# Uneven token chunks, four index-query jobs left out, and index keys gathered across sequences, in a fused sparse-attention and HGRN2 step

## The chip, the core and the metric

The kernel runs as one program on one core of a Trainium2 chip. The metric is the device time of one execution in microseconds (us); lower is better. The core has TensorE (PE, matrix products; PEld is its weight loading), VectorE (DVE), ScalarE (ACT), GpSimd (POOL) and the queues that issue DMA transfers (SP's above all). Each engine works through its own list of instructions in a fixed order and waits at semaphores.

## What is computed

One step of a one-layer decoder on 1024 prompt tokens and 8 sample tokens (one for each of 8 sequences with 1024 past keys). A normalised input goes through one wide projection; its columns feed sparse attention, an index that picks 256 keys for each query, and a gated linear recurrence (HGRN2). The part that matters here:

```python
def indexer_topk(iq, iw, ik, q_pos, topk):
    s = jnp.einsum('bthd,bsd->bths', iq.astype(F32), ik.astype(F32)) * IDX_DIM ** -0.5
    score = jnp.einsum('bths,bth->bts', jax.nn.relu(s), iw)
    ...
    score = jnp.where(causal[None], score, -jnp.inf)
    _, idx = lax.top_k(score, topk)          # topk = 256
    valid = idx <= q_pos[None, :, None]
    return idx, valid
```

A prompt query at position below 256 has at most 256 visible keys, so all of them are kept whatever their scores are: its index query is never used. The sample tokens' index queries are used, against keys that are gathered page by page from `cache_ik` through `page_table`.

## The kernel before, in words

**Units and jobs.** The 4168 columns of the projection are cut into 17 units of at most 256 columns (`UNITS`): unit 0 is `ix` (index keys and weights, 72 columns), units 1 and 2 are `iq` (index queries, 4 heads each), unit 3 is the first half of `gh`, unit 4 the first `hg` (gate and query of two HGRN2 heads), and so on. The weights of a unit arrive by DMA (`w_raw`), ACT writes their rounded high part (`high_w`, tile `w_high`), POOL the rest (`split_w`, tile `w_low`), and every product is three matrix products: high with high, high with low, low with high. PE works through *jobs*: one job is 24 matmuls (8 slices of the 1024 inputs, three products) into one PSUM bank. A job of form "T" has the columns of the projection on partitions and a *chunk* of tokens as its moving columns; form "N" has one row tile of 128 tokens on partitions and 256 columns of the projection moving; form "S" does the 8 sample tokens of the next unit (64 small matmuls). `ix`, `iq` and `hg` are computed in form T; an `iq` or `hg` unit has two halves `b` of 128 columns, each over the three chunks of `CHUNKS`.

**The front.** The input rows `x_rows` (9 tiles: 8 of 128 tokens and the sample tokens as tile 8) are loaded by SP. For each group of tiles ACT sums the squares (`squares`), DVE works out the roots in a chain of eleven small instructions (`x_roots`), DVE and ACT scale the rows (`scale_rows`), PE transposes them (`transpose_x`, L2150), ACT copies the high part out of PSUM (`high_x`) and DVE the low part (`low_x`). `X_AT` says within which job PE transposes which slices of the next chunk. `FRONT` lists the jobs of group 0, in which `ix` and the first `iq` unit alternate chunk by chunk. `IX_JOBS` is the number of jobs after which the last `ix` job is done: the weights of unit 2 take the place of those of unit 0, so `high_w(2)` waits for it.

**Index items.** An item (`ITEMS`) is one row tile t = 2 to 7 of queries, one head h: PE multiplies with all keys up to t (2 or 4 matmuls, L2214), ACT applies relu (`index_relu`), DVE weighs and adds to `scores` (`add_scores`). Two PSUM buffers and two relu buffers alternate. There are 48 items in 12 groups of four; `GROUPS` says behind which job a group is done: on PE its four items are spread over the job that follows. After all items and a causal mask on POOL (`affine_select`), DVE searches the 256th largest score bit by bit in 31 rounds; the loop that follows on DVE takes the sample tokens' search in between.

**POOL's list at the start** is: `split_w(0)`, `split_w(1)`, then the 32 gathers of index keys (`load_index_keys`: sequence pair `bp` = 0 to 3, page `g` = 0 to 7, 64 KB each) with `split_w(2)` and `split_w(3)` among them, then six causal masks, `split_w(4)` and the later units. Each gather waits until the one before it *of the same pair* has landed:

```python
for g in range(g0, g1):
    ge(gp, s[f"index_pages_in{bp}"], 16 * g)
```

PE begins a unit only when its whole low part is there:

```python
elif u not in begun:
    begun.add(u)
    pe.wait_ge(s["weights_low_ready"], 2 * u + 2)
```

A job also waits until the one that used its bank before has been copied out (`job_copied`). The product with the gathered keys (`sample_index`, L2240) is behind job `SAMPLE_AT`, the sum over heads (`sample_index_sum`, L2248) behind `SAMPLE_SUM_AT`. Later events (`FLAGS_AT`, `EVENTS` with the recurrence's chunks) are placed by job number too.

## Time and profile before

| | us |
|---|---|
| median of 3 runs (lowest, highest) | 805.73 (801.14, 806.96) |
| profiled execution, device time | 804.48 |
| its span, first to last instruction | 802.8 |
| PE busy | 760.7 |
| DVE busy | 542.8 |
| ACT busy | 420.7 |
| POOL busy | 396.2 |

The device time lies 1.7 us above the span; what is added to the span is added to it. A wait on an engine counts only where the chain that ends last passes through it.

### The profile page before, as it was taken

The page shows a single profiled execution, that of the slowest core. Times are in us where ns is not written, and L with a number is a line of the kernel's source. Part 1 is how long each engine was busy: PE and PEld are TensorE (multiplying, and loading weights), DVE is VectorE, ACT ScalarE, POOL GpSimd, SP SyncE. Part 2 cuts the span into 40 slices and gives each one's busy share as a digit, 9 for nine tenths or more (in the row PEclk, how much of TensorE's full clock was granted, in tenths as well). Part 3 has the DMA queues.
Part 4 walks back from the last instruction along what each step waited for, and adds up shares of the span by engine and source line. Part 5 has one row for each costly group of instructions (what it writes and reads, how often), then busy time and mean ns, then how long its engine had stood idle before and what let it go on. Part 6 is the DMA issues. An engine that isn't in the chain of part 4 may idle for free.

```text
span 802.8 us, 20221 instructions
## 1 busy us (share of the span) xinstructions
PE 760.7 (95%) x7576; PEld 704.1 (88%) x7576; DVE 542.8 (68%) x1110; ACT 420.7 (52%) x1274; POOL 396.2 (49%) x576
## 2 busy tenths in 40 slices
PE   3999999999999999999989999979799998999998
PEld 3889989899999999999988999868588878898998
DVE  3644767998999999879994846678446367555121
ACT  6765775346365686577554746554435554422110
POOL 3454735437735693579396435249932427510220
PEclk9999999999999999999999999999999999999999
...
GB/s 282 93 21 86 14 90 41 66 66 42 53 3 80 94 47 74 80 95 47 74 28 75 124 127 166 161 253 134 155 153 140 206 122 142 124 139 55 229 101 82
DMA packets 69927, 83.57 MB, mean 104 GB/s; under 512 B 20458, under 2 KB 55962, under 8 KB 69578
## 3 DMA queue, kind: packets, MB, share of 16 engines
...
## 4 chain that ended last, share of the span: by engine, by line
PE 76%; POOL 8%; DVE 5%; issue 4%; ACT 4%; DMA 2%; POOLq 0%; SPq 0%; ACTq 0%; DVEq 0%
PE psum L2298 25%; PE psum L2295 16%; PE psum L1331 11%; PE psum L2214 3%; PE psum L1264 3%; PE psum L1280 3%; POOL w_low L549 2%; PE psum L2172 2%; PE psum L2191 1%; PE psum L1242 1%; PE psum L1238 1%; PE psum L2150 1%; PE psum L1244 1%; DMA page_keys<-in_cache_kt 1%; POOL page_keys L613 1%
## 5 line engine op out<-in xcount | busy, mean ns | idle before, releaser
L2298 PE MATMUL psum<-w_high,xT_high 128*128 128x256 f32 x640 | 183.2, 286 | 0.3 <-ACT stage L1804 0.3
L2298 PE MATMUL psum<-w_low,xT_high 128*128 128x256 f32 x640 | 179.8, 281 | 0.0
L2298 PE MATMUL psum<-w_high,xT_low 128*128 128x256 f32 x640 | 179.6, 281 | 0.0
L549 POOL TENSOR_TENSOR w_low<-w_raw,w_high 128x256 fp32r<-128x256 f32 (+1 forms) x144 | 105.5, 769 | 65.0 <-ACT w_high L1686 54.7
L2298 PEld LDWEIGHTS psum<-w_high,xT_high 128*128 128x128 f32 x640 | 120.4, 188 | 2.4 <-ACT stage L1804 0.5
L2298 PEld LDWEIGHTS psum<-w_high,xT_low 128*128 128x128 f32 x640 | 120.5, 188 | 0.4
L2298 PEld LDWEIGHTS psum<-w_low,xT_high 128*128 128x128 f32 x640 | 120.6, 188 | 0.0
L2295 PE MATMUL psum<-xT_high,w_high 128*128 128x384 f32 (+3 forms) x312 | 103.8, 333 | 0.9 <-POOL w_low L549 0.9
L2295 PE MATMUL psum<-xT_high,w_low 128*128 128x384 f32 (+3 forms) x312 | 100.3, 322 | 0.0
L2295 PE MATMUL psum<-xT_low,w_high 128*128 128x384 f32 (+3 forms) x312 | 100.3, 322 | 0.0
L2037 DVE TENSOR_SCALAR_CACHE_REDUCE flag_count<-scores,candidate 128x512 f16<-128x512 f32 (+2 forms) x96 | 96.9, 1009 | 0.0
L2037 DVE TENSOR_SCALAR_CACHE_REDUCE flag<-scores,candidate 128x384 f16<-128x384 f32 (+2 forms) x96 | 84.1, 876 | 9.2 <-DVE candidate L2053 8.6
L914 ACT ACTIVATE prob<-psum,neg_max 128x1024 f32<-128x1024 f32 (+7 forms) x64 | 47.4, 740 | 67.6 <-DVE neg_max L1172 67.4
L1331 PE MATMUL psum<-w_high,xT_high 128*128 128x256 f32 x256 | 73.3, 286 | 0.1
L1331 PE MATMUL psum<-w_low,xT_high 128*128 128x256 f32 x256 | 71.9, 281 | 0.0
L1331 PE MATMUL psum<-w_high,xT_low 128*128 128x256 f32 x256 | 71.8, 281 | 0.0
L1576 POOL DMA_INDIRECT index_keys_T<-in_cache_ikt,index_page_rows x32 | 34.8, 1088 | 56.1 <-DMA index_keys_T<-in_cache_ikt,index_page_rows 54.8
L2295 PEld LDWEIGHTS psum<-xT_high,w_high 128*128 128x128 f32 (+1 forms) x312 | 58.4, 187 | 3.7 <-POOL w_low L549 1.4
L2295 PEld LDWEIGHTS psum<-xT_low,w_high 128*128 128x128 f32 (+1 forms) x312 | 58.3, 187 | 0.7
L1172 DVE CUSTOM_DVE_ANT_0 psum<-psum,mask 128x1024 f32<-128x1024 f32 (+5 forms) x48 | 43.0, 898 | 23.5 <-PE psum L1244 23.3
L2295 PEld LDWEIGHTS psum<-xT_high,w_low 128*128 128x128 f32 (+1 forms) x312 | 58.1, 186 | 0.5
L1804 ACT ACTIVATE stage<-psum 128x256 f32<-128x256 f32 x64 | 24.7, 387 | 57.6 <-PE psum L2298 53.5
...
## 6 DMA issues: line engine op xcount, KB each, us to landing
...
```

The source lines that it names most:

```text
L549: last = gp.tensor_tensor(WL[:, u % 2, 4 * h + k, 0:w], raw(u)[:, h, k, 0:w], f(WH[:, u % 2, 4 * h + k, 0:w]), ALU.subtract)
L914: act.activation(PB[:, m % 3, 0:w], ps(2 * (m % 2), w), ACT.Exp, scale=-1.0, bias=NB[:, h:h + 1], accum_out=RS[:, t % 2, h:h + 1]).then_in ...
L1172: dve.tensor_tensor_reduce(lg, lg, mask, -HD ** -0.5, 3e38, ALU.add, ALU.min, accum_out=NB[:, h:h + 1])\
L1264: last = pe.transpose(ps(4, P, o=b * P), PB[:, m % 3, b * P:(b + 1) * P], IDN[:, :])
L1280: last = pe.matmul(ps(7, P, (g + 1) * HD, g * HD, kv * P), VT[:, b, kv * HD:(kv + 1) * HD], PTS[(2 * p + g) % 3][:, b, :], start=b == 0, s ...
L1331: last = pe.matmul(ps(OBANK[y], UW, rows(i)), a[:, k, row0(i):row0(i) + rows(i)], ww[:, sl, k, :], start=k == 0 and a is XH and ww is WH, ...
L1576: gp.indirect_dma_start(dst, None, cache_ikt.rearrange("a d k -> (a d) k"), bass.IndirectOffsetOnAxis(ap=PGX[:, col:col + 1], axis=0))\
L1804: last = act.activation(STG[0:r, (g + 1) % 4, :], ps(bank, UW, r), fn)
L2037: dve.tensor_scalar((JK, CU)[k % 2][:, 0:w], sc, threshold(k), None, op, ALU.add, accum_out=CNT[:, k:k + 1]).then_inc(s["dve_chain"], 1)
L2214: last = pe.matmul(ps(4 + 2 * (m % 2) + c0 // 512, w), IQS[:, h, (t - 2) * P:(t - 1) * P], stack[:, c0:c0 + w], start=kk == 0, stop=kk == 1)
L2295: last = pe.matmul(ps(BANK[n], cw, m_), ww[:, sl, k, i * P:i * P + m_], x[:, k, t0:t0 + cw], start=first, stop=final)
L2298: last = pe.matmul(ps(BANK[n], w, rows(i)), x[:, k, row0(i):row0(i) + rows(i)], ww[:, sl, k, 0:w], start=first, stop=final)
```

## The change

`CHUNKS` goes from 384, 384 and 264 tokens (the last with the 8 sample tokens) to 256, 384 and 392. The row tiles are grouped 2, 3 and 4 (`CHUNK_ROWS`), with one tile of each group scaled by ACT. The first chunk now holds only tokens whose index queries are never used, so `FRONT` and the `iq` unit skip it: four jobs of 24 matmuls fewer, jobs 2 lower in number after the front and 4 lower after unit 2. All tables of job numbers are moved; `GROUPS` starts behind job 6 instead of 8. `sample_index` is behind job 20 instead of 22, which is now the first job of unit 4 and was the seventh of unit 3. All tiles of the second chunk are transposed in one go behind job 0. SP loads the second group of rows ahead of the weights of unit 1. POOL's gathers are in another order: pages 0 to 2 of the pairs 0, 1, 2 in turn; after `split_w(2)` pages 0 to 2 of pair 3; then pages 3 to 7 of all four pairs in turn; `split_w(3)` behind them all.

```diff
@@ -51,7 +51,9 @@
-CHUNKS = [(0, 384), (384, 384), (768, 264)]
+CHUNKS = [(0, 256), (256, 384), (640, 392)]
+CHUNK_ROWS = [(0, 1), (2, 3, 4), (5, 6, 7, 8)]
+ROWS_BY_ACT = (1, 4, 7)
 UNITS = [("ix", 0), ("iq", 0), ("iq", 1), ("gh", 0), ("hg", 0), ("hv", 0), ("hv", 1),
@@ -83,11 +85,11 @@
-FRONT = [(x, b, c) for c in range(3) for x, b in ((0, 0), (1, 0), (1, 1))]
-IX_JOBS = 7
+FRONT = [(x, b, c) for c in range(3) for x, b in ((0, 0), (1, 0), (1, 1)) if x == 0 or c > 0]
+IX_JOBS = 5
 SAMPLE_UNITS = [u for u in range(3, NU) if UNITS[u][0] != "hg"]
...
-X_AT = {(2, 3): (1, range(4)), (2, 7): (1, range(4, 8)), (4, 7): (2, range(4)), (5, 3): (2, range(4, 8))}
+X_AT = {(0, 7): (1, range(8)), (3, 3): (2, range(4)), (3, 7): (2, range(4, 8))}
@@ -102,7 +104,7 @@
     if kind == "iq":
-        out = [(u, "T", b, c) for c in range(3) for b in range(2)]
+        out = [(u, "T", b, c) for c in (1, 2) for b in range(2)]
         return out + [(u + 1, "S", NT, 0)] if u == 2 else out
@@ -121,25 +123,25 @@
     JOB0.append(JOB0[-1] + len(jobs(_u)))
-LOWS = JOB0[2] + 6
+LOWS = JOB0[2] + 4
 ORDERED = [job for _u in range(NU) for job in jobs(_u)]
...
 ITEMS = [(t, 4 * half + h) for half in range(2) for t in range(2, NT) for h in range(4)]
-GROUPS = {8: [0], 9: [1], 10: [2], 11: [3], 12: [4], 13: [5, 6], 15: [7], 16: [8], 17: [9], 18: [10], 19: [11]}
+GROUPS = {6: [0], 7: [1], 8: [2], 9: [3, 4], 11: [5], 12: [6], 13: [7], 14: [8], 15: [9], 16: [10], 17: [11]}
 ITEMS_AT = {n: [4 * g + x for g in gs for x in range(4)] for n, gs in GROUPS.items()}
-KEYS_ROWS_AT, SAMPLE_AT, SAMPLE_SUM_AT = 7, 22, 23
-
-FLAGS_AT = {29: 0, 36: 1, 42: 2, 46: 3, 49: 4, 53: 5, 72: 6, 77: 7}
+KEYS_ROWS_AT, SAMPLE_AT, SAMPLE_SUM_AT = 5, 20, 21
+
+FLAGS_AT = {25: 0, 32: 1, 38: 2, 42: 3, 45: 4, 49: 5, 68: 6, 73: 7}
 KEEP_AT = [4, 6, 8, 10, 12, 14, 23, 26]
...
-    chunk = t // 3
-    return max(IX_JOBS, (3, 6, 9)[chunk] if h < 4 else JOB0[2] + 2 * chunk + 2)
+    c = 1 if t < 5 else 2
+    return max(IX_JOBS, (4, 7)[c - 1] if h < 4 else JOB0[2] + 2 * c)
@@ -1436,15 +1438,15 @@
             def load_x(g):
-                for i in range(3 * g, 3 * g + 3):
+                for i in CHUNK_ROWS[g]:
                     sp.dma_start(x_buf(i)[0:rows(i)], x_rows(i)).then_inc(s[f"x_in{i}"], 16)
...
             sp.dma_start(LG[:, :], bass.AP(ln_g.tensor, 0, [[1, P], [P, KC]]), allow_slow_non_contiguous=True).then_inc(s["gain_in"], 16)
+            load_x(1)
             load_weights(sp, 1)
-            load_x(1)
             load_x(2)
@@ -1565,11 +1567,9 @@
-            def load_index_keys(bp, g0, g1):
-
-                if bp == 3:
-                    gp.wait_ge(s["x_transposed"], 2 * KC)
-                for g in range(g0, g1):
+            def load_index_keys(g0, g1, bps):
+
+                for g, bp in [(g, bp) for g in range(g0, g1) for bp in bps]:
                     ge(gp, s[f"index_pages_in{bp}"], 16 * g)
@@ -1581,26 +1581,23 @@
                 link(gp.iota(ROWN[hh * HD:(hh + 1) * HD, :], [[0, SB // 2 * NPG]], base=0, channel_multiplier=1))
-            gp.wait_ge(s["x_rows_scaled"], 2)
             split_w(gp, 0)
...
             link(gp.tensor_tensor(PGX[:, :], PGX[:, :], ROWN[:, :], ALU.add))
-            load_index_keys(0, 0, NPG)
+            load_index_keys(0, 3, range(3))
             gp.wait_ge(s["const_in"], CONSTS_IN)
...
             gp.tensor_scalar(TRI[:, P:2 * P], TRF[:, :], 1.0, 0.0, ALU.mult, ALU.add)
-            load_index_keys(1, 0, 3)
             gp.wait_ge(s["x_low_ready"], 3 * KC)
...
             split_w(gp, 2)
-            load_index_keys(1, 3, NPG)
-            load_index_keys(2, 0, 3)
+            gp.wait_ge(s["x_transposed"], 3 * KC)
+            load_index_keys(0, 3, (3,))
+            load_index_keys(3, NPG, range(4))
             split_w(gp, 3)
-            load_index_keys(2, 3, NPG)
-            load_index_keys(3, 0, NPG)
             for u in range(2, NU):
@@ -1653,7 +1650,7 @@
-                act.wait_ge(s["x_roots_ready"], i // 3 + 1)
+                act.wait_ge(s["x_roots_ready"], ROWS_BY_ACT.index(i) + 1)
                 act.activation(x_buf(i), x_buf(i), ACT.Copy, scale=STAT[:, 3, i:i + 1]).then_inc(s["x_rows_scaled_act"], 1)
@@ -1768,7 +1765,7 @@
                                     iqp[b2 * HD:(b2 + 1) * HD, 8 * b2 + 2 * j + hh:4 * BR:BR + 16],
-                                    ps(bank, SB, (hh + 1) * HD, hh * HD, 256)[:, b2:SB:2], ACT.Copy)
+                                    ps(bank, SB, (hh + 1) * HD, hh * HD, T - t0)[:, b2:SB:2], ACT.Copy)
                 elif kind == "ix":
@@ -1841,16 +1838,16 @@
             act.activation(RS[:, 0, 0:1], CNT[:, 0:1], ACT.Square)
-            for i in range(3):
+            for i in range(2):
                 squares(i)
             high_w(0)
-            scale_rows(2)
+            scale_rows(1)
             act.wait_ge(s["gain_in"], 16)
-            high_x(0, range(4))
+            high_x(0, range(KC))
+            for i in range(2, 5):
+                squares(i)
             high_w(1)
-            high_x(0, range(4, KC))
-            for i in range(3, 6):
-                squares(i)
+            scale_rows(4)
             for u in (0, *range(2, NU)):
@@ -1859,25 +1856,22 @@
                     if n == 1:
-                        for i in (6, 7):
+                        for i in range(5, NT + 1):
                             squares(i)
-                        scale_rows(5)
-                    if n == 2:
-                        squares(NT)
+                    if n == IX_JOBS - 1:
+                        high_w(2)
                     if (n, 3) in X_AT:
...
                     evac(u, q)
-                    if n == 3:
+                    if n == 1:
                         scale_rows(7)
...
                         high_w(u + 1)
-                    if n == IX_JOBS - 1:
-                        high_w(2)
                     if n == KEYS_ROWS_AT:
@@ -1931,8 +1925,8 @@
             def x_roots(g):
-                c = slice(3 * g, 3 * g + 3)
-                dve.wait_ge(s["x_squares_ready"], 3 * g + 3)
+                c = slice(CHUNK_ROWS[g][0], CHUNK_ROWS[g][-1] + 1)
+                dve.wait_ge(s["x_squares_ready"], CHUNK_ROWS[g][-1] + 1)
                 x, y, tmp = STAT[:, 1, c], STAT[:, 3, c], STAT[:, 2, c]
@@ -2071,27 +2065,26 @@
             x_roots(0)
-            for i in (0, 1):
-                scale_rows(i)
+            scale_rows(0)
             dve.wait_ge(s["gain_in"], 16)
...
             x_roots(1)
-            for i in (3, 4):
+            for i in (2, 3):
                 scale_rows(i)
...
                         low_x(*X_AT[n, 3])
+                    if n == 1:
+                        x_roots(2)
+                        for x in (5, 6, NT):
+                            scale_rows(x)
                     if n < LOWS:
...
                     if n == 2:
-                        x_roots(2)
-                        for x in (6, NT):
-                            scale_rows(x)
-                    if n == 4:
                         constants()
@@ -2140,12 +2133,12 @@
                     pe.wait_ge(s["ident_in"], 16)
-                pe.wait_ge(s["x_rows_scaled"], 2 * c + 2)
+                pe.wait_ge(s["x_rows_scaled"], (1, 3, 6)[c])
                 pe.wait_ge(s["x_rows_scaled_act"], c + 1)
...
                         pe.wait_ge(s["x_low_ready"], KC * c + k - 3 if c > 0 else 1)
-                    for i in range(3 * c, 3 * c + 3):
+                    for i in CHUNK_ROWS[c]:
                         r = rows(i)
```

POOL at the start of the program, from its first `split_w` (`w_low`) on. `x8` is one `split_w`; `index_keys_T_140` is the tile of pair 3. Before:

```order
L549 TENSOR_TENSOR w_low<-w_raw,w_high 128x72 x8
L549 TENSOR_TENSOR w_low<-w_raw_146,w_high 128x256 x8
...
L1576 DMA index_keys_T<-in_cache_ikt,index_page_rows 128x128 x8
...
L1576 DMA index_keys_T<-in_cache_ikt,index_page_rows 128x128 x3
L1597 TENSOR_TENSOR x_sample_T<-xT_high,xT_low 128x64
L549 TENSOR_TENSOR w_low<-w_raw,w_high 128x256 x8
L1576 DMA index_keys_T<-in_cache_ikt,index_page_rows 128x128 x8
L549 TENSOR_TENSOR w_low<-w_raw,w_high 128x256 x8
L1576 DMA index_keys_T<-in_cache_ikt,index_page_rows 128x128 x5
L1576 DMA index_keys_T_140<-in_cache_ikt,index_page_rows 128x128 x8
L1611 AFFINE_SELECT scores<-scores 128x128 x6
```

And now, from the same place:

```order
L1576 DMA index_keys_T<-in_cache_ikt,index_page_rows 128x128 x9
...
L1595 TENSOR_TENSOR x_sample_T<-xT_high,xT_low 128x64
L551 TENSOR_TENSOR w_low<-w_raw,w_high 128x256 x8
L1576 DMA index_keys_T_140<-in_cache_ikt,index_page_rows 128x128 x3
L1576 DMA index_keys_T<-in_cache_ikt,index_page_rows 128x128 x3
L1576 DMA index_keys_T_140<-in_cache_ikt,index_page_rows 128x128
...
L551 TENSOR_TENSOR w_low<-w_raw,w_high 128x256 x8
L1608 AFFINE_SELECT scores<-scores 128x128 x6
L551 TENSOR_TENSOR w_low<-w_raw,w_high 128x256 x16
```

Between `split_w(2)` and `split_w(3)` stood 8 gathers and now stand 23; none is left behind `split_w(3)`.

PE from the last index item (t = 7, 4 matmuls) to the start of unit 4, whose first job is the one that waits for `weights_low_ready`. Before:

```order
686 L2214 MATMUL psum<-ikT_high_low_144,iqT_stack_143 128x512 [waits index_relu_ready,index_low_ready]
...
693 L2298 MATMUL psum<-w_high_113,xT_high_102 128x256 [waits job_copied]
...
744 L2240 MATMUL psum<-index_keys_T_180,iq_padded_181 64x512 [waits index_pages_in1]
...
753 L2298 MATMUL psum<-w_high_113,xT_high_102 128x256 [waits job_copied]
...
777 L2248 MATMUL psum<-relu_sample_182,index_weight_sel_97 128x512 [waits index_weights_selected,sample_index_relu]
...
780 L2295 MATMUL psum<-xT_high_102,w_high_113 128x384 [waits job_copied,weights_low_ready]
```

And now:

```order
638 L2207 MATMUL psum<-ikT_high_low_144,iqT_stack_143 128x512 [waits index_relu_ready,index_low_ready]
...
645 L2291 MATMUL psum<-w_high_113,xT_high_102 128x256 [waits job_copied]
...
669 L2288 MATMUL psum<-xT_high_102,w_high_113 128x256 [waits job_copied,weights_low_ready]
...
696 L2233 MATMUL psum<-index_keys_T_180,iq_padded_181 64x512 [waits index_pages_in1]
```

Between the last item's rest of a job and unit 4 stood three jobs, `sample_index` and its sum; now one job stands there, and the other two jobs are ahead of the last item.

## Rows read from the trace of the kernel before

**Rows 1.** The page: the chain that ended last, by engine.

```profile
PE 76%; POOL 8%; DVE 5%; issue 4%; ACT 4%; DMA 2%; POOLq 0%; SPq 0%; ACTq 0%; DVEq 0%
```

**Rows 2.** Waits of PE, 0 to 160 us: in total, times, longest.

```profile
PE psum L2150 <- DVE x_rows L1950: 13.1, 1, 13.1
PE psum L2214 <- ACT relu L1834: 1.9, 4, 0.8
PE psum L2295 <- POOL w_low L549: 0.9, 2, 0.6
```

**Rows 3.** The chain in order of time, 0 to 160 us: start, duration, what.

```profile
34.45 8.38 PE psum L2295 x48
42.84 1.94 PE psum L2150 x12
...
54.27 0.26 issue
...
62.07 0.80 PE psum L2295 x3
...
64.67 0.35 PE psum L2214 x2
...
76.67 0.64 PE psum L2214 x4
...
88.70 0.81 PE psum L2214 x4
...
134.06 0.93 PE psum L2214 x4
134.99 6.04 PE psum L2298 x51
```

**Rows 4.** Timeline, 0 to 55 us: start, duration, instruction, [idle before].

```profile
5.67 1.06 ACT L1651 ACTIVATE square_junk<-x_rows 128x1024 bf16<-128x1024 f32 x1
...
9.36 0.17 DVE L1937 TENSOR_SCALAR x_stats<-x_stats 128x3 f32<-128x3 f32 x1 [7.81 <-ACT square_junk L1651]
...
11.54 1.15 ACT L1657 ACTIVATE x_rows<-x_rows,x_stats 128x1024 f32<-128x1024 f32 x1 [1.64 <-DVE x_stats L1942]
11.54 1.42 DVE L1950 TENSOR_SCALAR x_rows<-x_rows,x_stats 128x1024 f32<-128x1024 f32 x2
...
13.06 5.34 PE L2150 MATMUL psum<-ident,x_rows 128*128 128x128 f32 x24 [13.06 <-DVE x_rows L1950]
...
18.07 0.51 PE L2295 MATMUL psum<-xT_high,w_high 128*72 128x384 f32 x1
...
43.88 1.59 ACT L1664 ACTIVATE xT_high<-psum,ln_gain 128x264 fp32r<-128x264 f32 x4
```

**Rows 5.** Timeline of POOL, 45 to 140 us and from 128 us.

```profile
76.36 0.94 POOL L1576 DMA_INDIRECT index_keys_T<-in_cache_ikt,index_page_rows  x1 [1.75 <-DMA index_keys_T<-in_cache_ikt,index_page_rows]
77.61 0.94 POOL L1576 DMA_INDIRECT index_keys_T<-in_cache_ikt,index_page_rows  x1 [0.31 <-issue]
80.27 1.25 POOL L1576 DMA_INDIRECT index_keys_T<-in_cache_ikt,index_page_rows  x1 [1.71 <-DMA index_keys_T<-in_cache_ikt,index_page_rows]
...
84.17 9.60 POOL L549 TENSOR_TENSOR w_low<-w_raw,w_high 128x256 fp32r<-128x256 f32 x8
...
137.77 5.59 POOL L549 TENSOR_TENSOR w_low<-w_raw,w_high 128x256 fp32r<-128x256 f32 x8
```

**Rows 6.** Groups of POOL by shape, 20 to 135 us: the gathers.

```profile
L1576 POOL DMA_INDIRECT index_keys_T<-in_cache_ikt,index_page_rows x32 | 34.8, 1088 | 56.1 <-DMA index_keys_T<-in_cache_ikt,index_page_rows 54.8 <-issue 1.1 <-POOL index_page_rows L1589 0.3
```

**Rows 7.** Timeline of PE, 574 to 590 us, around a wait for a DMA.

```profile
579.36 1.93 PE L1358 MATMUL psum<-page_keys,q_padded 128*32 128x256 f32 x16 [4.36 <-DMA page_keys<-in_cache_kt]
...
583.95 0.41 PE L1242 MATMUL psum<-bias_high,antidiagonal_r 128*128 128x256 f32 x1
584.16 0.42 PE L1242 MATMUL psum<-bias_low,antidiagonal_r 128*128 128x256 f32 x1
```

**Rows 8.** Stretches of 3 us: busy time of PE, PEld, DVE, ACT, POOL, then granted clock, DMA share, GB/s.

```profile
582.00:585.00 3.00, 3.00 (x15) 2.46 (x17) 0.62 (x2) 0.60 (x1) 0.00 (x0) 0.52 0.09 23
```

## The prediction

> **What bounds the kernel now.** First the page's chain: PE carries 76% of it, POOL 8% [rows 1]. Then PE's waits in the first 160 us, where the change lies: one of 13.1 us at the start, 1.9 us for relus, 0.9 us for POOL's low weights [rows 2]. So after the start PE runs through, and what counts is PE's own work plus any wait that the change makes. The last reading is the chain in order of time [rows 3], which gives PE's pace and two marks. Pace: 48 matmuls of 384 columns in 8.38 us are 0.175 us each; 51 of 256 columns in 6.04 us are 0.118 us. So columns are paid for, at (0.175 - 0.118)/128 = 0.00045 us each, and one of 392 will take 0.178 us. A job is 24 of them: 2.8 us at 256, 4.2 at 384, 4.3 at 392. Marks: the last `ix` job ends at 54.3 us, and the seventh job of unit 3 at 141.0 us (134.99 + 6.04) [rows 3].
>
> **The removed jobs and the new widths.** Four jobs of 24 matmuls are gone. The chunks still sum to 1032 columns, so the `hg` units cost what they did (two jobs of 0.175 us and one of 0.12 before; one each of 0.118, 0.175 and 0.178 now, within 0.1 us a half). The `iq` units lose 256 columns in each of four halves: 4 x 24 x 0.118 = 11.3 us of PE's work. That is the gain on offer, and what follows takes it back.
>
> **The front.** Durations from [rows 4]. The first two tiles' squares end at 6.8 us. The roots take 2.2 us (9.36 to 11.54), the scaled row 1.15 us: PE's transposes start at 10.2 instead of 13.1 us. ACT copies 8 slices of 256 columns at 0.4 us (four of 264 in 1.59) to 14.2. Now the cover is missing: before, three jobs of the first chunk (12.6 us) lay over the squares, roots and scales of the next tiles; now one 256-column job does. Three squares (1.24 us each) end at 18.0, `high_w(1)` goes beside the roots (20.2), the two DVE scales end at 21.6. PE waits some 4 us for that. The 24 transposes then take 5.0 us if they run as the first 24 did (13.06 to 18.07), 2.9 us at the pace of the sixteen in 1.94 us [rows 3]; I take the slow one, as PE comes out of a wait in both: 26.6. Job 1 ends at 30.8, jobs 2 and 3 at 39.2, with two blocks of 16 transposes (1.94 us each) 43.1, and the last `ix` job at J = 47.4 us. Before it was 54.3 with two more jobs (8.4 us) ahead of it, so the front itself has lost 1.5 us. POOL's low weights of unit 1 are ready near 25 us, ahead of job 2. Bounds for this: 2.1 us less with quick transposes, 3 us more if a landing is late.
>
> **From J to unit 3, on PE.** Jobs 5 and 6 take 8.6 us and the transposed index rows between them 1.6 (54.27 to 62.07 less two jobs of 5.9 us and a wait of 0.3). `high_w(2)` and `split_w(2)` need 1.1 + 5.6 us and are covered by these 10.2. Unit 2 has two jobs of 384 and two of 392 columns, 17.0 us. One item costs 0.35 us at t = 2, 0.64 at t = 4, 0.81 at t = 6 and 0.93 at t = 7 [rows 3]; the sizes step evenly, so four heads of t = 2 to 6 are 11.8 us. The S job adds 1.0, small products 0.2, and 0.7 us goes where ACT copies a 392-column job ahead of the relus. PE asks for unit 3 at J + 10.2 + 17.0 + 11.8 + 1.9 = J + 40.9.
>
> **The same stretch on POOL.** `split_w(2)` ends at J + 6.7. Three gathers of pair 3 follow one after another; a gather alone is 0.94 us of issue and 1.75 us until it lands, 2.7 to 2.8 us [rows 5], so J + 13.4. Then 20 gathers over four pairs. Their waits are for a gather issued four earlier, so I take them as hidden: the pair at 76.36 and 77.61 overlapped, the second landed as soon as if alone [rows 5]. What is left is the issue, 1.09 us in the mean of 32 [rows 6], and 0.31 us between two [rows 5]: 1.36 us with the 1.05 of this stretch, 27.2 us together, J + 40.6. `split_w(3)` takes 5.6 us where DVE does not add scores (137.77) and 9.6 where it does (84.17) [rows 5]. PE's stall lets DVE run dry, so 5.7: J + 46.3. PE waits 5.4 us. The gathers' own waits, some 50 us of POOL's [rows 6], were off the chain in the kernel before, so taking them away earns nothing by itself; moving 15 more gathers ahead of `split_w(3)` is what counts. Ends: 0 if a gather takes 1.0 us, 13 us if each takes 1.55 and the split 9.6.
>
> **The clock after a wait.** After a wait of 4.36 us PE's 256-column matmuls start 0.21 us apart (583.95, 584.16) [rows 7], and the granted clock up to 585 us is 0.52, the level of 1.2 GHz [rows 8]. From 579.4 to 585 PE did about half of what 0.118 us a matmul gives, so such a wait costs some 2.5 us more. I add 2.5. The Trainium skill, "TensorE: Matmul & The Clock Gate", section "HAM oscillation — how this bites in real kernels", says that waits between bursts of matmuls put the array back to 1.2 GHz at each of them; by that rule both waits of this forecast pay, and the trace agrees with its 0.52.
>
> **Unit 3 to its seventh job.** PE starts at 47.4 + 46.3 = 93.7. Seven N jobs are 19.8 us, the items of t = 7 and of the second half 3.7 + 15.4, and 1.1 us is lost where `high_w(4)` (2.0 us) lies between two groups of relus on ACT. With 2.5 us for the clock: 136.2, against 141.0 before: 4.8 us ahead.
>
> **The start of unit 4.** `split_w(4)` is behind the causal masks, and these are behind the last scores. Before, the last item left PE at 134.99 and `split_w(4)` ended at 143.36 (137.77 + 5.59) [rows 3, 5]: 8.4 us, hidden by three jobs, `sample_index` and its sum. Now only 27 matmuls of 256 columns, 3.2 us, are in between; PE waits 5.2 us, and 2.5 go to the clock. Ends: 3 us with no clock loss, 9 us if the masks come late. 4.8 - 7.7 = **2.9 us slower**. Beside it: `sample_index` moved two jobs later still finds all gathers landed (J + 41); the DVE search keeps its distance to PE within 0.5 us (two N jobs later, 5.2 us of wait), so flags, scans and the recurrence stay where they were; the shorter first `hg` job sits where POOL paces the recurrence, and I take 0, ends -2 and +2 us.
>
> **The sum** against the profiled execution: 804.5 + 2.9 = 807.4 us. The median of the three runs is 1.2 us above that execution, so I say **808 us**. A measurement tells about 1% (8 us) from no change.
>
> **Rivals.** (1) The gathers are quick or the front loses less, and `split_w(3)` is on time; unit 4 still waits. For it: 1.25 us a gather, the smallest seen, saves 2.2 of the 5.4 us, and below some length the wait may leave the clock up. 807.4 - 5.4 - 2.5 = 799.5 us. (2) Neither wait appears: 799.5 - 7.7 = 791.8 us. Against it stands that the span from last item to low weights is made of a relu, a score, a mask and eight subtractions, all of fixed length, so it needs PE itself to run later than I think. (3) Slower: DVE holds POOL up. It decides from about 5 us more on POOL. The split at 84.17 took 4.0 us longer beside the scores than the one at 137.77 [rows 5], and gathers issued there take up to 1.25 us and more; at 1.55 us a gather 20 of them are 3.8 us more. 807.4 + 4.0 + 3.8 = 815.2 us. Against it: scores end when PE stands. The Trainium skill, "SBUF — State Buffer", section "Who interferes with whom", says that a DVE instruction with two SBUF inputs contends with a GpSimd instruction that reads SBUF; the scores are of that kind, and the 9.6 against 5.6 us agrees. By it the long split is the one to take if scores are still running. (4) That the change doesn't do what it says is excluded: the order of instructions has the four jobs less.
>
> **How the numbers follow.** Forecast 0.50, rival 1 0.18, rival 2 0.14, rival 3 0.18. The range reaches from rival 1 less 1.5 us to rival 3: 798 to 815 us, leaving out rival 2 and little else. Faster by over 1% (under 797.7): rival 2 and a bit, 0.15. Slower by over 1% (over 813.8): rival 3 and the tail of the forecast, 0.21. Same: 0.64.
>
> **What would show it.** In PE's waits after the change: one on DVE's scaled rows after job 0 of about 4 us, one for `w_low` before unit 3 of 5 us and one before unit 4 of 5 us, each with a granted clock near 0.5 behind it; POOL's gathers 1.25 to 1.5 us apart with no waits for landing; the last `ix` job ending near 47 us, the seventh job of unit 3 near 136. Wrong would be: gathers that run one at a time in spite of the order (20 at 2.7 us put unit 3 27 us later and the time near 830), or an end of the items so late that `split_w(4)` is hidden.

## The result, and the profile after

The changed kernel takes **819.05 us** (median of 4 runs, 816.25 to 824.24), the kernel before 804.91 in the same session: ratio 1.0188, 95% interval 1.0144 to 1.0231. The forecast was 808 us with a range up to 815: wrong in size, and beyond its range. Every trace is of one execution. The executions of one kernel differ by some microseconds (here 5.8 us from fastest to slowest before, 8.0 us after), so marks inside one trace are compared to tenths of a microsecond, but whole times only by the medians and their intervals. The profiled execution has a span of 816.8 us (before 802.8). Its chain, and TensorE's waits over the whole span (in total, times, longest):

```profile
PE 60%; DVE 15%; issue 9%; POOL 6%; ACT 6%; another core or an unknown queue 2%; DMA 1%; SPq 0%; DVEq 0%; ACTq 0%; POOLq 0%
```

```profile
PE psum L2207 <- ACT relu L1831: 14.5, 5, 7.2
PE psum L2143 <- ACT x_rows L1654: 11.5, 1, 11.5
PE psum L2143 <- DVE x_rows L1944: 7.6, 1, 7.6
PE psum L2288 <- POOL w_low L551: 5.2, 1, 5.2
PE psum L2291 <- ACT psum L1806: 4.8, 3, 3.3
```

Against [rows 1] and [rows 2]: the one front wait of 13.1 us has become two, 19.1 us; the relus cost 14.5 us in place of 1.9; the wait for unit 4's low weights is there as forecast (5.2); the forecast one ahead of unit 3 is not.

**The front.** VectorE's roots and scales of the second chunk (timeline of DVE: start, duration):

```profile
20.00 0.16 DVE L1936 SCALAR_TENSOR_TENSOR x_stats<-x_stats 128x3 f32<-128x3 f32 x1
20.20 0.74 DVE L1934 TENSOR_TENSOR x_stats<-x_stats 128x3 f32<-128x3 f32 x1
20.97 0.65 DVE L1935 SCALAR_TENSOR_TENSOR x_stats<-x_stats 128x3 f32<-128x3 f32 x1
...
24.38 2.31 DVE L1944 TENSOR_SCALAR x_rows<-x_rows,x_stats 128x1024 f32<-128x1024 f32 x2
```

The same kind of instruction takes 0.16 us at 20.00 and 0.65 behind it: GpSimd's split of unit 1 starts at 20.19 and runs to 26.1. The two scales take 2.31 us where two took 1.42 [rows 4]. The split of unit 1 in the kernel before, then in the changed one:

```profile
17.50 5.59 POOL L549 TENSOR_TENSOR w_low<-w_raw,w_high 128x256 fp32r<-128x256 f32 x8 [1.99 <-ACT w_high L1686]
```

```profile
20.19 5.95 POOL L551 TENSOR_TENSOR w_low<-w_raw,w_high 128x256 fp32r<-128x256 f32 x8 [10.24 <-ACT w_high L1683]
```

Both times it starts on ScalarE's `high_w(1)`. In the kernel before that stood ahead of the squares of the second group, and the split was over at 23.1, just ahead of the second group's roots at 23.80. The change puts it behind the squares, and the split now runs beside the roots.

**The hole.** ScalarE, then GpSimd, in the items of unit 2:

```profile
80.40 0.70 ACT L1831 ACTIVATE relu<-psum 128x640 f32<-128x640 f32 x1 [1.17 <-PE psum L2207]
89.57 0.70 ACT L1831 ACTIVATE relu<-psum 128x640 f32<-128x640 f32 x1 [8.46 <-remote]
98.08 1.30 ACT L1831 ACTIVATE relu<-psum 128x640 f32<-128x640 f32 x2 [7.80 <-remote]
```

```profile
79.96 0.94 POOL L1576 DMA_INDIRECT index_keys_T<-in_cache_ikt,index_page_rows  x1 [0.30 <-issue]
81.21 0.95 POOL L1576 DMA_INDIRECT index_keys_T<-in_cache_ikt,index_page_rows  x1 [0.30 <-issue]
...
93.72 0.94 POOL L1576 DMA_INDIRECT index_keys_T<-in_cache_ikt,index_page_rows  x1 [0.31 <-issue]
94.69 6.15 POOL L551 TENSOR_TENSOR w_low<-w_raw,w_high 128x256 fp32r<-128x256 f32 x8
```

The relu at 89.57 needs the item's products (TensorE left them at 79.2) and a free relu buffer, that is the score two items back (VectorE, before 78). Both had long come, and "remote" says that the profile knows no releaser. The same at 98.08. All that went on was GpSimd's gathers, 1.25 us apart, with no wait between them. I call this stretch the hole. The stretches (busy time of PE, PEld, DVE, ACT, POOL, granted clock, DMA share, GB/s):

```profile
64.00:80.00 16.00, 16.00 (x89) 14.93 (x88) 8.92 (x20) 9.63 (x20) 10.15 (x11) 1.00 0.19 51
80.00:82.00 2.00, 1.12 (x8) 0.74 (x6) 0.99 (x2) 0.70 (x1) 1.70 (x2) 1.00 0.22 66
82.00:90.00 8.00, 1.25 (x8) 0.92 (x6) 0.00 (x0) 0.43 (x1) 5.87 (x8) 0.74 0.19 51
90.00:94.00 4.00, 3.58 (x10) 2.91 (x10) 0.88 (x1) 0.27 (x1) 3.08 (x4) 0.50 0.17 49
94.00:98.00 4.00, 0.00 (x0) 0.00 (x0) 0.00 (x0) 0.00 (x0) 3.98 (x6) 0.50 0.11 33
```

TensorE, VectorE and ScalarE all stand for most of 18 us; the granted clock falls to 0.50, its 1.2 GHz level. The DMA share stays between 0.11 and 0.22.

**Unit 4.** The chain in order of time:

```profile
154.03 1.30 DVE scores L1996
155.75 5.49 POOL w_low L551 x8
161.29 4.45 PE psum L2288 x24
```

The last score, the split behind the last mask, then unit 4: the wait of 5.2 us, as worked out.

### The profile page after: what moved, and what is told of

Its sections match the earlier page's. It is cut to its first block, busy times and chain, and to the rows that moved or that the text cites. A ratio compares the mean times of both kernels' runs of the same rounds, so it can differ in the third digit from the quotient of the medians.

```text
span 816.8 us, 20008 instructions
## 1 busy us (share of the span) xinstructions
PE 752.3 (92%) x7480; PEld 695.5 (85%) x7480; DVE 556.9 (68%) x1102; ACT 420.3 (51%) x1266; POOL 387.7 (47%) x576
## 4 chain that ended last, share of the span: by engine, by line
PE 60%; DVE 15%; issue 9%; POOL 6%; ACT 6%; another core or an unknown queue 2%; DMA 1%; SPq 0%; DVEq 0%; ACTq 0%; POOLq 0%
PE psum L2291 14%; PE psum L1333 11%; PE psum L2288 10%; PE psum L2207 4%; PE psum L1266 4%; PE psum L1282 3%; DVE flag_count L2031 3%; POOL w_low L551 2%; DVE bit_kept L2044 2%; DVE flag L2031 2%; PE psum L1240 1%; PE psum L1246 1%; PE psum L1244 1%; POOL w_low L560 1%
## 5 line engine op out<-in xcount | busy, mean ns | idle before, releaser
L551 POOL TENSOR_TENSOR w_low<-w_raw,w_high 128x256 fp32r<-128x256 f32 (+1 forms) x144 | 102.9, 755 | 70.5 <-ACT w_high L1683 70.5
L2288 PE MATMUL psum<-xT_high,w_high 128*128 128x392 f32 (+5 forms) x280 | 95.9, 342 | 5.2 <-POOL w_low L551 5.2
L2288 PE MATMUL psum<-xT_low,w_high 128*128 128x392 f32 (+5 forms) x280 | 92.4, 330 | 0.0
L2288 PE MATMUL psum<-xT_high,w_low 128*128 128x392 f32 (+5 forms) x280 | 92.2, 329 | 0.0
L916 ACT ACTIVATE prob<-psum,neg_max 128x1024 f32<-128x1024 f32 (+7 forms) x64 | 47.4, 741 | 67.8 <-DVE neg_max L1174 67.6
L1996 DVE SCALAR_TENSOR_TENSOR scores<-relu,index_weight,scores 128x384 f32<-128x384 f32 (+5 forms) x42 | 40.8, 972 | 30.6 <-ACT relu L1831 29.3
L2288 PEld LDWEIGHTS psum<-xT_high,w_high 128*128 128x128 f32 (+1 forms) x280 | 53.2, 190 | 7.5 <-POOL w_low L551 5.4
L1683 ACT ACTIVATE w_high<-w_raw 128x1024 fp32r<-128x1024 f32 (+1 forms) x42 | 41.3, 1026 | 27.9 <-DMA w_raw<-in_w_main 19.2
L1831 ACT ACTIVATE relu<-psum 128x384 f32<-128x384 f32 (+5 forms) x48 | 35.7, 759 | 38.1 <-PE psum L2207 19.2
L2288 PEld LDWEIGHTS psum<-xT_low,w_high 128*128 128x128 f32 (+1 forms) x280 | 53.2, 190 | 0.7
```

The costliest lines, as they stand in the source:

```text
L551: last = gp.tensor_tensor(WL[:, u % 2, 4 * h + k, 0:w], raw(u)[:, h, k, 0:w], f(WH[:, u % 2, 4 * h + k, 0:w]), ALU.subtract)
L916: act.activation(PB[:, m % 3, 0:w], ps(2 * (m % 2), w), ACT.Exp, scale=-1.0, bias=NB[:, h:h + 1], accum_out=RS[:, t % 2, h:h + 1]).then_in ...
L1683: act.activation(WH[:, u % 2, 4 * h:4 * h + 4, 0:w], raw(u)[:, h, :, 0:w], ACT.Copy)\
L1831: act.activation(RB[:, m % 2, 0:w], ps(4 + 2 * (m % 2), w), ACT.Relu).then_inc(s["index_relu_ready"], 1)
L1996: ins = dve.scalar_tensor_tensor(sc, RB[:, m % 2, 0:w], IW[:, t, h:h + 1], sc, ALU.mult, ALU.add)
L2288: last = pe.matmul(ps(BANK[n], cw, m_), ww[:, sl, k, i * P:i * P + m_], x[:, k, t0:t0 + cw], start=first, stop=final)
```

## The experiments

Sixteen kernels, in four sessions; each ratio is to the kernel before in the same session, with its 95% interval. "Changed" is the changed kernel. The letters name the theories that each expectation states.

**1. Is it the gathers?** Three kernels: pace them; give back their old order; or put the new order alone into the kernel before.

```
# one at a time: changed, in load_index_keys
+ if g > 2 and bp > 0:
+     gp.wait_ge(s[f"index_pages_in{bp - 1}"], 16 * (g + 1))
+ if g > 3 and bp == 0:
+     gp.wait_ge(s["index_pages_in3"], 16 * g)
# old order: changed, with load_index_keys called at the places and with the pages of the kernel before
# by three: before, with load_index_keys and its calls as in the changed kernel
```

> The changed kernel with one thing added: each of the 20 gathers behind the three also waits until the gather issued before it has landed, so that one is in flight at a time, in the same order. Theory G (the run of gathers, issued 1.25 us apart without a pause, starves ScalarE: its relu stood 8.5 and 7.8 us with both of its semaphores long reached): the two waits of TensorE of 7.2 and 4.9 us on relu vanish. The gathers then take about 20 x 2.8 = 56 us from 65, so the last is issued near 121 and the split of unit 3's weights ends near 127, some 13 us behind the end of unit 2 at about 110: a new wait for w_low of unit 3 of 10 to 15 us. Time 815 to 823 us, no gain, but with the hole moved from 80 to 98 us to the start of unit 3. Theory C (the hole comes from the order of ScalarE's and VectorE's work under the new chunks, whatever GpSimd does): the relu waits stay at 14.5 us in all, and the time is about 819 us or more.

> The changed kernel with the old order and places of the gathers: eight of pair 0, three of pair 1, split of unit 2, five of pair 1, three of pair 2, split of unit 3, then the other 13, each waiting for the one before of its pair as before. The chunks and the left-out index queries stay. Theory G: no hole between 80 and 98 us, TensorE's relu waits fall from 14.5 to under 4 us, no new wait for unit 3's w_low (split of unit 3 ends near 90 us, unit 3 asks near 108). Time 802 to 808 us, near the kernel before: the 11.3 us of work removed less the later front. Theory C: the hole stays and the time is 815 to 821 us.

> The kernel before with the gathers' new order alone (three pages of three pairs at once, then after the split of unit 2 three of the last pair and 20 back to back, then the split of unit 3). Chunks and jobs as before. Theory G: the run of 20 lies at about 66 to 94 us, a hole of 8 to 16 us on ScalarE appears there and the time is 812 to 822 us. Theory C: no hole; split of unit 3 ends near 100 us, before it is wanted, and the time is 803 to 808 us as before.

Measured: one at a time 849.71 us (1.055, 1.0471 to 1.063); old order **805.72** (1.001, 0.9971 to 1.0049); by three alone **821.24** (1.0195, 1.0111 to 1.0279). TensorE's waits in the first 210 us with one at a time, and with the old order:

```profile
PE psum L2295 <- POOL w_low L551: 45.4, 1, 45.4
...
PE psum L2292 <- POOL w_low L551: 5.2, 1, 5.2
PE psum L2211 <- ACT relu L1835: 1.0, 1, 1.0
```

```profile
PE psum L2146 <- ACT x_rows L1657: 11.6, 1, 11.6
PE psum L2146 <- DVE x_rows L1947: 7.0, 1, 7.0
PE psum L2291 <- POOL w_low L551: 5.1, 1, 5.1
PE psum L2210 <- ACT relu L1834: 1.6, 2, 0.9
```

Paced or in the old order there is no hole. With the gathers' order alone on the kernel before, ScalarE stands as in the changed one:

```profile
88.27 0.70 ACT L1830 ACTIVATE relu<-psum 128x640 f32<-128x640 f32 x1 [4.99 <-remote]
93.20 0.48 ACT L1758 ACTIVATE iqT_stack<-psum 64x384 fp32r<-64x384 f32 x1 [4.22 <-remote]
...
100.94 1.51 ACT L1830 ACTIVATE relu<-psum 128x768 f32<-128x768 f32 x2 [6.76 <-remote]
```

So the gathers' order costs some 16 us alone, and the chunks with the left-out queries neither cost nor gain anything measurable. Theory G (the gathers do it) holds, and theory C (the order of work under the new chunks) is dead. My 815 to 823 for one at a time was far too low: a gather took 3.4 us in the mean from issue to issue, not 2.8, and TensorE, with no hole, asked for unit 3 at 94 us, not 110, so that the wait was 45.4 us and not 10 to 15.

**2. The front.** The split of unit 1 on GpSimd held back.

```
  split_w(gp, 0)
+ gp.wait_ge(s["x_rows_scaled"], 3)
  split_w(gp, 1)
```

> The changed kernel with the split of unit 1's weights on GpSimd held until the rows of group 1 are scaled, as it was held before the change. Theory P (GpSimd's split slows VectorE's small root instructions, 0.66 to 0.75 us each instead of 0.17, so the rows of the second chunk come at 26.7 us instead of 21.6): roots are back at 0.2 us, the rows are scaled near 22 to 23 us, TensorE's wait of 7.6 us falls to 3 to 4 us, and the time falls by 2 to 5 us, to 814 to 817. Rival: the split only moves later and unit 1's low weights come late, or the hole between 80 and 98 us takes up what is gained: time within 1 us of 819.

Measured: 817.15 us (1.0118, 1.0042 to 1.0193).

```profile
20.25 0.16 DVE L1935 TENSOR_TENSOR x_stats<-x_stats 128x3 f32<-128x3 f32 x1
...
21.43 1.42 DVE L1945 TENSOR_SCALAR x_rows<-x_rows,x_stats 128x1024 f32<-128x1024 f32 x2
```

The roots are back at 0.16 us, the scales at 1.42, the rows ready at 22.9 in place of 26.7; the wait is 4.9 us in place of 7.6, and the second chunk's jobs start at 28.3 us in place of 31.7. Theory P (the split slows VectorE's roots) holds for the place. The kernel's gain of 1.9 us is inside its scatter. The expectation calls this hold the one of the kernel before, and that is not so: there the split waited only for the first chunk's rows, scaled at 13.0 us [rows 4], and was early by ScalarE's order.

**3. What of the gathers makes the hole: landing, number, rate, bytes?**

```
# two in flight: changed, for the 20 gathers (g0 == 3)
+ if g0 == 3 and n > 1:
+     gp.wait_ge(s[f"index_pages_in{run[n - 2][1]}"], 16 * (run[n - 2][0] + 1))
# eight, split, twelve: changed
- load_index_keys(3, NPG, range(4)); split_w(gp, 3)
+ load_index_keys(3, 5, range(4)); split_w(gp, 3); load_index_keys(5, NPG, range(4))
# split first: changed, with split_w(gp, 3) ahead of the 23 late gathers
# plain copies: changed, for g > 2; the rows come from fixed places, so the page table is left out
- gp.indirect_dma_start(dst, None, ...)
+ gp.dma_start(dst, cache_ikt.rearrange("a d k -> (a d) k")[col * P:(col + 1) * P, :])
# spaced: changed, behind each of the 20
+ link(gp.tensor_scalar(ANR[:, :], ANT[:, :], 1.0, 0.0, ALU.mult, ALU.add))
```

> The changed kernel with each of the 20 gathers waiting until the gather two places before it has landed: two in flight where the changed kernel has up to four unwaited, and the run with one in flight had one. From the run with one in flight a gather takes about 3.25 us from issue to the next, so two in flight should come 1.6 to 2.0 us apart, 20 of them in 32 to 40 us, split of unit 3 ending near 108 to 114 us. Theory G1 (it is the rate of 1.25 us that starves ScalarE, and 1.6 to 2.0 us is slow enough): no idle stretch of ScalarE over 3 us with both semaphores reached; TensorE waits 12 to 20 us for w_low of unit 3 instead; time 820 to 828. Theory G2 (any gathers in flight while ScalarE works through the items do it): the hole stays and w_low is late too; time 825 to 840.

> The changed kernel with the split of unit 3's weights put into the run of gathers behind the first eleven (three of the last pair and eight), so that no run is longer than twelve. In the changed kernel and in the two others with the run of 20, ScalarE's first late start came after some 6 to 10 gathers of the run, and the nine gathers at 27 to 38 us made none. Theory G3 (the length of the run decides: something fills up over about ten gathers and empties in a pause): little or no hole, TensorE's waits on relu in all under 4 us, no wait for w_low of unit 3; time 804 to 809. Theory G4 (each gather costs ScalarE, wherever it is): the hole is cut in two parts of 6 to 8 us each and the time stays 815 to 820.

> The changed kernel with the split of unit 3's weights ahead of all 23 late gathers. The run of gathers then starts some 10 to 14 us later (near 75 to 80 us) and keeps its pace of 1.25 us. Theory G: the hole moves with the run, to some 88 to 108 us, and stays 12 to 16 us in all, in whichever items stand there; time 814 to 820 us. Theory C (something in the program of ScalarE at item 9 to 11 of the 24, not the gathers' time): the hole stays at items 9 to 11 near 80 to 98 us. If the gathers reach into the stretch where VectorE masks and sums the scores, the affine masks and the split of unit 4 are as late as before (wait of 5.2 us).

> The changed kernel with the 20 gathers of the run replaced by plain copies of as many bytes (128 rows of 512 B, 64 KB) issued by the same engine with the same waits; the rows come from fixed places instead of the index pages, so that the sample's index scores are computed from other pages. Theory D (the traffic of 64 KB per 1.25 us, 52 GB/s, or the DMA engines' share of 0.2 starves ScalarE): the hole stays, 815 to 820 us. Theory Q (GpSimd's own work of making the descriptors of an indirect gather does it, not the bytes): no hole; TensorE waits under 4 us on relu, the split of unit 3 starts earlier if a plain copy is issued faster than 1.25 us; time 803 to 808 us.

> The changed kernel with a small copy of 128x128 on GpSimd behind each of the 20 gathers (its duration was 0.32 us, with its completion awaited perhaps 0.45), which waits for nothing that a gather does: gathers some 1.7 us apart, as in the run with two in flight (35 us for 20, 1.75 each), but with no wait for a landing. Theory R (the rate of issue makes the hole: at 1.25 us ScalarE starved, at 1.75 it did not): no hole, and the split of unit 3 is late by some 8 to 14 us instead: time 812 to 817. Theory F (the number of gathers not yet waited for makes it, since only waits for a landing have removed it so far): the hole is there, of 8 us or more, and the time is 820 to 828.

| kernel | us | ratio, 95% interval | ScalarE's longest idle time with "remote" | TensorE's wait for unit 3's w_low |
|---|---|---|---|---|
| two in flight | 816.75 | 1.0166 (1.0094 to 1.0238) | 0.4 | 14.8 |
| eight, split, twelve | 809.18 | 1.0073 (1.0031 to 1.0116) | 7.3 | none |
| split first | 820.77 | 1.0209 (1.0126 to 1.0292) | 16.2 | none |
| plain copies | 806.71 | 1.0022 (0.998 to 1.0065) | none | none |
| spaced | 819.51 | 1.0204 (1.018 to 1.0228) | none | 15.4 |

Four of the five times missed the ranges of the theories that their traces bear out: two in flight came below 820 to 828, and eight, split, twelve, split first and spaced came 0.2, 0.8 and 2.5 us above theirs. What decides between the theories below is the hole in the trace, not the time.

Spaced, GpSimd's timeline: 1.8 us from gather to gather in the mean, and no gather waits for another to land.

```profile
81.08 0.98 POOL L1576 DMA_INDIRECT index_keys_T<-in_cache_ikt,index_page_rows  x1 [0.27 <-POOL antidiagonal_r L1580]
82.08 0.48 POOL L1580 TENSOR_SCALAR antidiagonal_r<-antidiagonal 128x128 fp32r<-128x128 f32 x1
82.84 0.98 POOL L1576 DMA_INDIRECT index_keys_T<-in_cache_ikt,index_page_rows  x1 [0.27 <-POOL antidiagonal_r L1580]
```

No hole, so it is the rate and not the count in flight (theory R over F), and two in flight (1.77 us in the mean) agrees. Plain copies, issued by the same engine to the same software queue, 20 in 13.4 us, bring more traffic at once and no hole:

```profile
64.00:80.00 16.00, 16.00 (x89) 14.92 (x88) 9.73 (x21) 10.64 (x22) 11.47 (x19) 1.00 0.33 90
80.00:100.00 20.00, 19.34 (x165) 16.99 (x164) 14.15 (x16) 15.05 (x30) 9.62 (x12) 1.00 0.20 61
```

So neither the bytes nor the queue by itself is it (Q over D); that it is the making of descriptors, as Q has it, no run isolates. One doubt stays: the copies were over in 13.4 us, and the gathers began to slow ScalarE and TensorE only some 8 to 13 us into a run, so a cause that goes by time and not by number is not excluded by this kernel. Splitting first moves the run to 82.8 to 110.2 us, and the hole moves with it, off the items where it was in the changed kernel. ScalarE, then TensorE, whose small matmuls (64 in 1.01 us in the chain of "one at a time") now come in handfuls every 0.72 us with nothing to wait for:

```profile
95.64 1.28 ACT L1799 ACT_TABLE_LOAD   x1
113.11 0.90 ACT L1799 ACTIVATE stage<-psum 8x64 f32<-8x64 f32 x4 [16.19 <-remote]
```

```profile
94.48 0.32 PE L2280 MATMUL psum<-w_raw,x_sample_T 128*8 128x64 f32 x4 [0.41 <-issue]
95.23 0.30 PE L2280 MATMUL psum<-w_raw,x_sample_T 128*8 128x64 f32 x4 [0.42 <-issue]
95.97 0.27 PE L2280 MATMUL psum<-w_raw,x_sample_T 128*8 128x64 f32 x3 [0.44 <-issue]
...
101.70 0.39 PE L2280 MATMUL psum<-w_raw,x_sample_T 128*8 128x64 f32 x3 [0.45 <-issue]
```

ScalarE's copy at 113.11 needs the last of these small matmuls, at 102.1. So of its 16.2 us of idle time 5.2 went on TensorE's own slowness, and it started 11.0 us late.

The length counts too. In "eight, split, twelve" the first nine in a row, the last issued at 77.8 us, cost nothing; in the twelve from 86.3 on, ScalarE stood from 96.4 until 103.67, 1.5 us behind the last. That is G3 (the length of the run) over G4 (each gather costs), with a run of twelve already too long.

**4. What was mended did not arrive.** From the old order: the split of unit 1 held; the split of unit 4 ahead of the last mask (`split_w(gp, u + 1)` at `t == NT - 1`, ahead of its wait); both.

> The kernel with the new chunks and the old order of gathers, with the split of unit 1 held until the rows of the second chunk are scaled. Theory P (in the run with the hold alone the rows were ready 3.8 us sooner, the wait of 7.6 us fell to 4.9, and the last index job of the front ended 3.2 us sooner; the kernel's time fell by only 1.9 us, inside its scatter): with no hole and no wait for unit 3's weights behind it, the 3 us arrive at unit 3's end; but unit 4 waits for its w_low by VectorE's scores (5.1 us). If VectorE's scores follow TensorE's earlier items, the whole moves: 802 to 803.5 us against 805.7. Rival: VectorE or ScalarE bounds the items and the 3 us are lost: 805 to 806.

> The kernel with the new chunks and the old order of gathers, with the split of unit 4's weights moved ahead of the last causal mask. The split then stands behind the fifth mask at 134.4 us and ends near 140.0, where unit 3's last job ends at 139.7; the last mask comes some 1 us later. Theory S (the wait of 5.1 us for w_low of unit 4, with a slower clock behind it, is time lost to the end): it falls to under 1 us and the time by 5 to 6 us, to 799.5 to 801. Rival (the search of the top keys on VectorE, which waits for the last mask, or a later wait takes it back): 803 to 806.

> The new chunks and the left-out index queries with the old order of gathers, the split of unit 1 held until the rows of the second chunk are scaled, and the split of unit 4 ahead of the last mask. If both gains add (3 and 5.5 us) the time is 796.5 to 799 us, 6 to 9 us under the kernel before, ratio 0.989 to 0.993. Rival: the gathers, which end at 131 us in the old order and stand ahead of the masks and of the split of unit 4, take the front's 3 us back, and the time is 799.5 to 801.

Measured: 806.42 (1.0044, 1.0028 to 1.0061), 807.67 (1.0066, 1.0041 to 1.0092), 809.52 (1.0072, 1.0042 to 1.0102). All three missed, and came out slower than even their rivals had it (806, 806 and 801 at most). Held, eleven gathers, nearly each behind the landing of the one before, stand between the split of unit 1 and that of unit 2, and TensorE waits 4.3 us for unit 2's low weights. With the split of unit 4 ahead of the mask, its wait is gone, but the split now runs beside the last four scores. These took 1.28 us each in the old order and take 10.90 together here (GpSimd and VectorE):

```profile
132.79 5.60 POOL L551 TENSOR_TENSOR w_low<-w_raw,w_high 128x256 fp32r<-128x256 f32 x8
```

```profile
132.75 10.90 DVE L2000 SCALAR_TENSOR_TENSOR scores<-relu,index_weight,scores 128x1024 f32<-128x1024 f32 x4 [0.57 <-ACT relu L1835]
```

So the last mask and VectorE's search come late, the search at 144.12 in place of 139.39, and TensorE waits for it. With all three it is the same (four scores in 10.89 us) and the search starts at 147.60:

```profile
144.12 0.55 DVE L2035 TENSOR_SCALAR_CACHE_REDUCE flag<-scores 128x384 f16<-128x384 f32 x1 [0.48 <-POOL scores L1613]
```

```profile
PE psum L2251 <- DVE enough L1001: 3.2, 3, 1.9
PE psum L2251 <- ACT hv L1796: 2.1, 1, 2.1
```

**5. Does the search set the time?** Short runs of gathers, with the splits between; items packed to end two jobs sooner, on three kernels.

```
# short runs: changed, with the split of unit 1 held
+ load_index_keys(3, 5, range(4)); split_w(gp, 3)
+ load_index_keys(5, 7, range(4)); split_w(gp, 4)      # no longer behind the masks
+ load_index_keys(7, NPG, range(4))
# early items: changed chunks
+ GROUPS = {6: [0], 7: [1], 8: [2], 9: [3, 4], 11: [5, 6], 12: [7], 13: [8, 9], 14: [10], 15: [11]}
# early items: kernel before
+ GROUPS = {8: [0], 9: [1], 10: [2, 3], 11: [4], 12: [5], 13: [6, 7], 15: [8, 9], 16: [10], 17: [11]}
```

> The changed kernel with GpSimd's queue mended in three places: the split of unit 1 held until the second chunk's rows are scaled; the run of 20 gathers cut into 8, 8 and 4 with the splits of unit 3 and of unit 4 between them; so no split behind the last mask. In every run so far VectorE's search began some 0.5 us behind the last mask, and the state updates of unit 6 on TensorE began 79 to 81 us behind it (before 137.84 to 216.8, old order 139.39 to 220.5, changed 155.79 to 235.7), whatever TensorE had gained or lost. Theory V (the end of the items sets the search's start and with it the time; no hole, no waits for w_low): items end 3 us sooner than with the old order, search begins near 136 to 137 us, time 800 to 803. Theory T (TensorE's own work sets the time): the 5.1 us for unit 4's w_low and 3 us of the front both arrive and the time is 796 to 798.

> The kernel with short runs of gathers, with the items also packed so that they end two jobs sooner (behind the job 15 in place of 17: two groups of four in one job twice). Theory V: items end some 5 to 6 us sooner (a job of unit 3 is 24 matmuls of 0.118 us, 2.8 us), search begins near 131 us, and the time falls by as much, to 795 to 798. Theory T, or ScalarE and VectorE cannot keep up with eight items in a job: no gain over the run without it, 800 to 803.

> The kernel before, with one thing changed: its items packed to end two jobs sooner (behind job 17 in place of 19). No work is taken away. Theory V: items end near 129 us in place of 135; the gathers, which end at 131.4 us ahead of the masks, let the search begin near 135 in place of 137.84, and the time falls by 2 to 3 us, to 800.5 to 802 against 803.5. Theory T: no change, within 1 us.

> The new chunks with the old order of gathers, and the items packed to end two jobs sooner. Theory V: the items end near 132 us in place of 138.9, the gathers end at 131.4, the search begins near 135.5 in place of 139.39, and the split of unit 4 ends near 141 in place of 144.8, so that TensorE waits 1 to 2 us for it in place of 5.1: the time falls by about 4 us from 805.7, to 801 to 803. Theory T: the wait for w_low alone counts, which falls by 3 to 4 us: about the same time, but then the early items of the kernel before gain nothing.

Measured: short runs **800.39** (0.9921, 0.9886 to 0.9956); with early items **799.34** (0.9927, 0.9896 to 0.9958); the kernel before with early items 803.92 (1.0002, 0.9978 to 1.0026); old order with early items 800.91 (0.996, 0.9933 to 0.9988). The first two are faster than the kernel before by 0.7 to 0.8%, the last by 0.4%; the early items add nothing measurable to the short runs. Marks of the profiled executions, in us: start of the last product of the index sum (TensorE), first flag of the search (VectorE), first product of the state updates (TensorE), span.

| kernel | sum | search | updates | span |
|---|---|---|---|---|
| before | 149.8 | 137.84 | 216.8 | 802.8 |
| before, early items | 152.7 | 135.35 | 219.7 | 801.9 |
| changed | 175.9 | 155.79 | 235.7 | 816.8 |
| old order | 160.7 | 139.39 | 220.5 | 805.7 |
| old order, early items | 157.7 | 138.69 | 217.5 | 799.1 |
| old order, split 4 early | 152.8 | 144.12 | 218.3 | 803.0 |
| all three of part 4 | 156.2 | 147.60 | 221.8 | 807.8 |
| short runs | 151.6 | 138.29 | 211.8 | 800.0 |
| short runs, early items | 154.2 | 135.15 | 213.9 | 794.8 |

Theory V (the search's start sets the time) falls as I had put it. On the kernel before the search starts 2.5 us sooner and the updates come 2.9 us later, as the sum does: TensorE sets them, 67.0 us behind the sum in both. In the new chunks (two jobs of unit 4 ahead of the sum) the distance is 59.7 to 59.8 us in four rows, and in the eight traces of such kernels that are not in the table. The two rows with the early split break it, at 65.5 and 65.6: there the updates come 74.2 us behind the search. So the updates start at about the later of sum + 59.8 and search + 74, a rule read off these marks and resting on two rows for its second half. Short runs stand on the edge (by the sum 211.4, by the search 212.3; found 211.8), with a visible wait for the search and one for ScalarE behind it:

```profile
PE psum L2294 <- ACT psum L1809: 3.9, 1, 3.9
PE psum L2250 <- DVE enough L1001: 3.6, 2, 2.7
```

From the updates to the end the rows differ by 7.3 us (580.9 to 588.2) with the same work. In the traces stand waits like these two, the one for `page_keys` (4.4 us before [rows 7], 3.5 in the old order, none in the changed kernel), with a slow clock behind them. These are single executions, and one kernel's own executions scatter as widely (short runs 791.31 to 807.0), so how much of this belongs to a kernel is not shown.

## Why the prediction was wrong, point by point

- **The removed jobs, 11.3 us:** right. TensorE has 96 matmuls less (x7480, before x7576).
- **The front, J = 47.4:** wrong, 53.6 measured (two jobs from 49.28 take 8.70 us, and it is the first). The step that failed is "the two DVE scales end at 21.6": they ended at 26.7, which is 5.1 of the 6.2 us. The forecast itself laid `high_w(1)` beside the roots and the low weights of unit 1 "near 25 us", so that the split ran across the roots and the scales, and it charged nothing for that. With the split held back the rows were ready at 22.9, so 3.8 us are the split's. The other 1.3 us came from the first chunk: its roots took 0.26 us each beside the split of unit 0, and its transposes began at 11.5 instead of 10.2. Another 0.9 us is a misreading: [rows 3] show 12 transposes in 1.94 us, and I took them for sixteen; the two blocks of sixteen took 2.38 us each. The Trainium skill, "SBUF — State Buffer", section "Who interferes with whom", says that VectorE contends with GpSimd's reads in an instruction with two SBUF inputs, and in tensor_scalar when it runs in its 2-port mode. The trace agrees for the first with 0.16 against 0.65 us; a tensor_scalar scale rose from 0.71 to 1.16, but no trace says in which mode it ran. I had used that rule for the long split only.
- **20 gathers on POOL:** the pace was 1.25 us, not 1.36, and none of the 20 waited; of the three ahead of them the first took 4.6 us until the next was issued, not 2.8. The split ended at 100.8, J + 47.2, against J + 46.3, so GpSimd's sum was right within 1 us. "PE waits 5.4 us" for unit 3 did not occur, since the hole made TensorE later than the split. By estimate it would have been some 7 us: one at a time, without a hole, TensorE asked for unit 3 at 93.9.
- **The step that failed for most of the miss:** the gathers' own waits were taken off as harmless ("taking them away earns nothing by itself"), at a price of nothing. They had spaced the gathers, and a run of some twenty without a pause stops ScalarE and TensorE. The old order against the changed kernel says what it costs: 15.2 us at the state updates, in place of my 7.9 us for unit 3's wait. At the seventh job of unit 3, ahead of the clock's share, it is 16.2 us (it ends at 153.3, and J + 83.5 is 137.1). No rival of mine had it. The third one, in which GpSimd is held up, came nearest in time (815.2) for another reason.
- **Unit 4's wait of 5.2 us:** right, 5.2. Its clock term of 2.5: the first job behind it took 4.45 us for 2.8, so 1.6; in the old order 5.49, so 2.7.
- **Unit 2 to the seventh job of unit 3:** some 2.6 us too short. Without waits I had J + 80.9; the old order gives J + 83.5. Which of its terms was too small I have not looked up.
- **"Flags, scans and the recurrence stay where they were":** in this execution wrong by 5 us the other way: 581.1 us from the updates to the end, before 586.0. The wait for `page_keys` (4.4 us) and the slow clock behind it are gone, the recurrence waits 1.4 us less, and TensorE waits 4.8 us more for ScalarE's copies. I had the first in my own rows and took it for fixed. That a part of these 5 us is scatter is not excluded.

To the updates: +6.2 (front) + 8.3 (hole 16.2 for 7.9) + 2.6 - 0.9 (clock) = 16.2; found 16.0 (235.7 against 216.8 + 2.9). With -4.9 behind them that is the miss of 11.1 us (818.5 against 807.4).

**Where the 11.3 us went without the hole.** Old order against before, at the updates: -11.3, +5.5 for the front waits (18.6 against 13.1), +2.7 for the second chunk's 24 transposes at the slow clock (5.27 us; in the kernel before two blocks of 12 took 1.31 us each), +5.1 for unit 4's low weights, +2.7 for the clock behind, -1.2 for other waits: +3.5, found +3.7. The end of the items did not move forward (last relu 136.57, before 135.02): they are tied to twelve consecutive jobs, and with four fewer ahead they reach two jobs further into unit 3, so the work between the last item and unit 4 shrank by some 12 us, about as much as was saved.

**Open:** how GpSimd's gathers reach ScalarE and TensorE. Both stood with every semaphore that the profile shows long reached, and TensorE's handfuls every 0.72 us look like a short supply of instructions or of semaphore updates. One packet of the instruction queues landed within the hole (82 to 84 us) and no other until 112; the kernel before also shows stretches of 20 us without one, so this settles nothing. Also open is whether the number of gathers or the length of the run in time decides, and why plain copies do nothing of the kind. No run here tells more.
